# State-space x of groups 1 to 7: 32x32 blocks on VectorE and 16 transfers instead of eight TensorE transposes

## What is computed

```
xbc = silu(causal_conv(u @ w_xbc))            # x (256 channels a group), B and C (128 each)
cb   = C B^T                                  # within chunks of 64 tokens
xdt  = x * dt ;  xte = xdt * decay_to_end     # by token and head
y    = (cb * decay) @ xdt + C @ state * exp(cum) + D * x
state = exp(cum_end) * state + B^T @ xte      # from chunk to chunk
y    = rmsnorm(y * silu(z)) per group, times ssm_norm
```

## Time and profile before

| | before |
|---|---|
| device time, median of 3 runs | 1791.07 us |
| device time of the profiled execution | 1791.04 us |
| its span, first to last instruction | 1789.3 us |
| TensorE busy in the span | 99% |
| VectorE busy in the span | 54% |
| chain that ended last | 99% TensorE |
| granted TensorE clock | 1.00 over the whole span |

### The profile page before, as it was taken

The page is one execution under the profiler, slowest core; times in us unless marked ns, Lnnn a source line. Parts: engine busy times, 40 slices in busy tenths (PEclk is TensorE's granted clock), DMA queues, the critical chain, the costliest instruction groups (busy, mean ns, idle before and its releaser), DMA issues.

```text
span 1789.3 us, 26607 instructions
## 1 busy us (share of the span) xinstructions
PE 1779.4 (99%) x9956; PEld 1499.2 (84%) x9956; DVE 969.1 (54%) x1407; ACT 633.9 (35%) x1002; POOL 89.3 (5%) x92
## 2 busy tenths in 40 slices
PE   9999999999999999999999999999999999999998
PEld 7888888888888888788988888888888888888887
DVE  6444443369999989623544455565334544444333
ACT  5222322244545444422333344443222332223221
POOL 2111100000000000000000000000000011111000
PEclk9999999999999999999999999999999999999999
DMA  5323323323344443233222322322332322233332
GB/s 173 105 94 100 100 94 105 105 94 97 95 106 100 102 104 92 84 106 103 86 71 71 104 72 93 94 93 71 97 103 94 95 94 94 94 101 99 106 105 71
DMA packets 84402, 172.98 MB, mean 97 GB/s; under 512 B 36800, under 2 KB 44224, under 8 KB 84336
## 3 DMA queue, kind: packets, MB, share of 16 engines
q1 hardware_dynamic: 76288, 162.83, 29.1%
q10 hardware_dynamic: 8048, 9.24, 2.4%
HBM read 166.21 MB, written 2.16 MB: 94 GB/s over the span
## 4 chain that ended last, share of the span: by engine, by line
PE 99%; DVE 0%; DMA 0%; issue 0%; SPq 0%; ACT 0%; DVEq 0%
PE G L583 50%; PE I L583 16%; PE G L650 13%; PE G L603 8%; PE I L1085 1%; PE I L1061 1%; PE G L908 1%; PE I L1051 1%; PE I L845 1%; PE I L710 1%; PE I L854 1%; PE I L831 1%; PE I L1021 0%; PE I L1025 0%; PE I L815 0%; PE I L836 0%
## 5 line engine op out<-in xcount | busy, mean ns | idle before, releaser
L1720 DVE TENSOR_TENSOR WL<-RAW,WH 128x1024 fp32r<-128x1024 f32 x296 | 372.2, 1261 | 287.9 <-ACT WH L1182 278.5
L1182 ACT CAST WH<-RAW 128x1024 fp32r<-128x1024 f32 x295 | 306.4, 1047 | 226.1 <-PE I L583 125.8
L583 PE MATMUL G<-UH,WH 128*128 128x512 f32 x664 | 164.3, 389 | 0.0
L583 PE MATMUL G<-UL,WH 128*128 128x512 f32 x664 | 164.0, 389 | 0.0
L583 PE MATMUL G<-UH,WL 128*128 128x512 f32 x664 | 164.0, 389 | 0.0
L583 PEld LDWEIGHTS G<-UL,WH 128*128 128x128 f32 x664 | 124.6, 188 | 25.9
L583 PEld LDWEIGHTS G<-UH,WL 128*128 128x128 f32 x664 | 124.6, 188 | 25.9
L583 PEld LDWEIGHTS G<-UH,WH 128*128 128x128 f32 x664 | 124.5, 188 | 25.8
L583 PE MATMUL G<-NH,WH 128*128 128x512 f32 x448 | 113.5, 395 | 0.0
L583 PE MATMUL G<-NL,WH 128*128 128x512 f32 x448 | 110.7, 389 | 0.0
L583 PE MATMUL G<-NH,WL 128*128 128x512 f32 x448 | 110.7, 389 | 0.0
(11 more groups left out here) (355 smaller groups left out, 2618.0 us busy)
## 6 DMA issues: line engine op xcount, KB each, us to landing
RAW<-in_slabs SPq DMA_DIRECT2D x296, 512.0 KB, 3.5
cum_rows<-kept_rows ACTq DMA_DIRECT2D x16, 256.0 KB, 7.0
SU<-y_turned SPq DMA_DIRECT2D x112, 32.0 KB, 2.7
bias<-in_rel ACTq DMA_DIRECT2D x16, 128.0 KB, 3.3
bias<-in_rel ACTq DMA_DIRECT2D x16, 112.0 KB, 2.8
h<-in_x SPq DMA_DIRECT2D x6, 256.0 KB, 5.9
out_y<-h SPq DMA_DIRECT2D x4, 256.0 KB, 2.5
h<-in_x ACTq DMA_DIRECT2D x2, 256.0 KB, 3.6
```

Of the source, the lines that this page charges most:

```text
L583: ins = mm(dst, slab(W, n)[:, (k - k0) * P:(k - k0 + 1) * P], R[:, k, :], start=begin and which == 0 and k == k0, stop=end and which == 2 ...
L1182: nc.scalar.copy(slab(WH, n), RAW[:, n.slot, :]).then_inc(split_hi, 1)
L1720: V.tensor_tensor(slab(WL, n), RAW[:, n.slot, :], slab(WH, n).bitcast(F32), ALU.subtract).then_inc(split_lo, 1)
```

## The change

- `turn_x`: in rounds 1 to 7 VectorE turns the 32x32 blocks of XT right behind the silu of t = 1 (two instructions, all 256 channels) into x_turned. `move_x`: SyncE moves them with 16 transfers into x_tokens, each of 32 partitions with one piece of 1 KB. Group 0 stays with TensorE.
- TensorE has the eight transposes of x for group 0 alone. XD on ScalarE and xte, xdt on VectorE read x_tokens in SBUF instead of I01 in PSUM; xte and xdt are made by two instructions each instead of one.
- y_turned is laid out so that a transfer of `move_y` also has one piece of 1 KB. They land in y_rows; ScalarE puts them in order with the gain into SU (two instructions) and copies SU to SH (two more). `ssm_hi` moves from t = 3 to t = 2.
- `ssm_lo` of groups 0 to 6 leaves VectorE: GpSimd subtracts SH from SU in one instruction of 128x1024. The last group stays on VectorE with a semaphore of its own.
- SyncE: the 16 transfers of x stand before the loads of slabs 8 and 9 of a round, the 16 of y in one piece behind them; before, the 16 of y stood in two halves with one load between.
- TensorE waits for WH before the first third and for WL only before the last one (`need_hi`, `need_slab`).

The diff, cut to its core:

```diff
+            def move_x(g):
+                sp.wait_ge(x_blocks, g)
+                for b in range(4):
+                    for q in range(4):
+                        sp.dma_start(x_tokens[32 * q:32 * q + 32, b], x_turned[32 * b:32 * b + 32, q]).then_inc(x_moved, 16)
...
             with sp.Fori(0, NG - 2) as i:
-                for j in range(1, 6):
+                for j in range(2, 6):
                     next_load(At(ahead + j, i, 6))
-                move_y(i + 1, (0, 1))
+                move_x(i + 2)
                 next_load(At(ahead + 6, i, 6))
-                move_y(i + 1, (2, 3))
+                next_load(At(ahead + 7, i, 6))
+                move_y(i + 1, (0, 1, 2, 3))
...
             def ssm_turn(g):
...
+                if isinstance(g, int) and g == 0:
+                    for j in range(TT):
+                        for f in range(2):
+                            nc.tensor.transpose(I01[:, j * 256 + f * P:j * 256 + (f + 1) * P],
+                                                XT[:, f, j * P:(j + 1) * P], ident[:])
...
             def fm(dst, n, RH, RL):
+                need_hi(n)
+                blocks(dst, n, 0, KT, RH, RL, True, False, (0, 1))
                 need_slab(n)
-                blocks(dst, n, 0, KT, RH, RL, True, True).then_inc(slab_done, 1)
+                ins = blocks(dst, n, 0, KT, RH, RL, False, True, (2,))
+                ins.then_inc(slab_done, 1)
...
+            def turn_x(g):
+                dve.wait_ge(sems["conv_done"], after("conv_done", g, 1))
+                dve.wait_ge(x_moved, 256 * (g - 1))
+                dve.wait_ge(sems["x_copied"], after("x_copied", g - 1))
+                for f in range(2):
+                    ins = V.transpose(x_turned.rearrange("p q (j f) c -> p f j q c", f=2)[:, f],
+                                      XT[:, f, :].rearrange("p (j q c) -> p j q c", q=4, c=32))
+                ins.then_inc(x_blocks, 1)
...
+            def ssm_lo(g, at=0):
+                pool.wait_ge(sems["ssm_hi"], last("ssm_hi", g))
+                pair = bass.ds(2 * g, 2)
+                ins = nc.gpsimd.tensor_tensor(SL[:, pair, :], SU[:, bass.ds(2 * (g + at), 2), :], SH[:, pair, :].bitcast(F32), ALU.subtract)
+                ins.then_inc(sems["ssm_lo"], 2)
...
                 if not first:
-                    ssm_lo(inner - 1)
                     group_gain(inner)
```

More of the change, by code:

```diff
@@ L542, in _ @@
             norm(1)
-            with pool.Fori(0, NG - 1) as i:
+            ssm(0)
+            with pool.Fori(1, NG - 1) as i:
+                ssm_lo(i - 1)
                 ssm(i)
+            ssm_lo(NG - 2, 1)
             ssm(NG - 1)
-            pool.wait_ge(sems["ssm_lo"], last("ssm_lo", NG - 1))
+            pool.wait_ge(ssm_lo_end, 2)
             nc.gpsimd.memset(RM[:], 1.0).then_inc(gk_pool, 1)
@@ L648, in tm_tile @@
                         if j == 0 and which == 0 and k == 4:
+                            need_hi(n + 1)
+                        if j == 0 and which == 2 and k == 0:
+                            need_slab(n)
+                        if j == 0 and which == 2 and k == 4:
                             need_slab(n + 1)
@@ L1345, in ssm_copy_exp @@
             def ssm_copy_exp(g, n=None):
-                act.wait_ge(sems["xb_turned"], after("xb_turned", g))
+                initial = isinstance(g, int) and g == 0
+                if initial:
+                    act.wait_ge(sems["xb_turned"], after("xb_turned", g))
+                else:
+                    act.wait_ge(x_moved, 256 * g)
                 act.wait_ge(sems["ssm_y"], last("ssm_y", g - 1))
@@ L1478, in ssm_round @@
                         decays(0)
+                    if t == 2 and not first:
+                        ssm_hi(inner - 1)
                     if t == 3:
-                        if not first:
-                            ssm_hi(inner - 1)
                         ssm_squares(inner)
@@ L2038, in ssm_x @@
             def ssm_x(g):
[L2039 to L2044 removed]
+                initial = isinstance(g, int) and g == 0
+                if initial:
+                    dve.wait_ge(sems["x_copied"], after("x_copied", g))
+                else:
+                    dve.wait_ge(x_moved, 256 * g)
+                dve.wait_ge(sems["u_done"], last("u_done", g - 1))
+                for dst, k, name in ((XTE, 2, "xte_ready"), (XDT, 1, "xdt_ready")):
+                    if k == 1:
+                        dve.wait_ge(sems["intra_done"], last("intra_done", g - 1))
+                    if initial:
+                        ins = V.tensor_tensor(dst[:].rearrange("p j (r c) -> p (j r) c", c=CH), heads(I01[:]), rows(k),
+                                              ALU.mult)
+                    else:
+                        for s in range(2):
+                            by_tile = gsc[:, 4 * k:4 * k + 4, :].rearrange("p j (f s) -> p s (j f)", s=2)[:, s, :]
+                            ins = V.tensor_tensor(
+                                dst[:].rearrange("p j (f s b c) -> p s b (j f) c", f=2, s=2, c=32)[:, s],
+                                x_tokens[:, 2 * s:2 * s + 2],
+                                by_tile.unsqueeze(1).unsqueeze(3).to_broadcast([P, 2, 2 * TT, 32]), ALU.mult)
+                    inc(ins, name)
+            def turn_x(g):
+                dve.wait_ge(sems["conv_done"], after("conv_done", g, 1))
+                dve.wait_ge(x_moved, 256 * (g - 1))
+                dve.wait_ge(sems["x_copied"], after("x_copied", g - 1))
+                for f in range(2):
+                    ins = V.transpose(x_turned.rearrange("p q (j f) c -> p f j q c", f=2)[:, f],
+                                      XT[:, f, :].rearrange("p (j q c) -> p j q c", q=4, c=32))
+                ins.then_inc(x_blocks, 1)
             def ssm_cb(g):
```

91 lines of the change are left out of this document (51 added, 40 removed).

## The result

| | before | after |
|---|---|---|
| median of the runs, us | 1790.97 (1790.86 to 1791.34, 5 runs) | 1801.47 (1798.91 to 1803.04, 5 runs) |
| ratio to before | | 1.0057, 95% interval 1.0046 to 1.0069 |
| profiled execution, span, us | 1791.04, 1789.3 | 1801.47, 1799.7 |

The account below looks back on a forecast made before the run. VectorE's ring, 41.2 us a round, was to replace TensorE's 40.65 us as the bound. The terms +1.4 - 1.6 - 0.3 - 0.8 = -1.3 us gave 1789.7 us, with a range of 1784 to 1800 (its own 1787.5 to 1793).

Parts of the forecast that it names:

- SyncE's issue: SyncE, 32 transfers a round instead of 16: 0.42 us each and 0.05 between, 16 in 7.5 us.
- The cover for slab 10: Load behind y's transfers: lands about 0.6 us after ScalarE would take it, VectorE needs it 3.6 us after that.
- my rival for late slabs: SyncE: 0.61 us a transfer, 16 take 11.7; slab 10 lands 1.6 us late, six times: 1799 us, chance 0.06.
- The port: GpSimd's subtraction asks before VectorE's silu, which stands 2.3 us: six rounds 1803.5 us, 0.14; round 7 alone 1792, 0.04.
- VectorE's ring: VectorE's state-space round: 41.35 - 1.63 (remainder) + 1.30 (blocks of x) + 0.15 (xte, xdt) = 41.2 us, the new bound.
- TensorE's round: State product to state product: 41.52 us on average, 40.65 without the x transposes, which take 0.87 us.
- Round 1, +1.4: Round 1 gets the blocks of x and longer xte, xdt but loses no remainder: its xdt comes 1.4 us later.
- The end, -0.8: Behind the last group: TensorE's 0.79 us wait for the seventh remainder goes, 0.8 us.
- The last segment, -0.3: Before the seventh group's product: VectorE gives 1.63 - 1.30 = 0.3 us.
- ScalarE at no cost: Two more copies of 0.6 us and the move to t = 2 fit ScalarE's idle time; nothing on the path.
- Split waits at no cost: TensorE waits for no slab in this stage, so nothing to win; the added, already met waits cost nothing.
- The full gain: Rival: VectorE's ring is looser, TensorE's 0.87 us come through seven times, and the 0.79: 1784.1 us; full or most, 0.16.

Follow-up runs that it names:

- the version with both repairs: Changed kernel with y's transfers halved around slab 10's load and GpSimd's subtraction held until the silu of t = 1: 1787.94 us, ratio 0.9985.

## Why the prediction was wrong, point by point

The sum priced two things at nothing: slab 10 behind the transfers of y ("Cover: this slack"), and GpSimd's subtraction beside VectorE. Together they cost 13.5 us, from 1787.94 to 1801.47.

- **SyncE's issue, the step that failed first.** I took 0.42 us for a transfer with one piece a partition, by the slabs' 333 and the weight rows' 420 ns, and held the 608 ns of y's transfers to be the price of their eight pieces. It is 0.59 us with one piece. I had priced by the number of pieces, from rows that differed in more than that: the cheap ones come from DRAM and go to 128 or 16 partitions, those of y go from SBUF to SBUF in 32. What sets the price stays open. In the trace before, transfers from SBUF to DRAM take 0.34 to 0.44 us (medians), and one from DRAM to SBUF, issued by ScalarE, takes 0.62:

```profile
L1281 ACTq DMA_DIRECT2D cum_rows<-kept_rows x16: 602/622/728, 414.5 to 660.8; - x16
```

- **The cover for slab 10.** Its load is issued 10.65 us after the first transfer of y where I had 7.5, and VectorE stands 0.87 to 1.1 us for it. So the cover was some 2.1 us; my rival for late slabs, where 4.2 us more left 1.6, had counted with 2.6. That rival also had 11.7 us for sixteen transfers, though its own 0.61 and 0.05 make 10.6, close to what was measured. Its 1799 stood for 1.6 us a round and no collision; its cost alone was 5.2 us.
- **The port: mechanism right, place not to be had.** That the silu would stand if GpSimd asked first, and by about 2.3 us (2.2 measured), was right. No run shows the 2.3 us of its sum as such: the silu stood 2.16 us (2.85 against 0.69), and the subtraction takes 2.36 to 2.42 us unblocked, against 1.30 for half of it. That block transposes and taps leave GpSimd alone holds: in the version with both repairs the subtraction takes 2.36 to 2.38 us beside them, and they take 1.30 to 1.31 and 2.27 to 2.28 us, as without it (1.30 and 2.27 with the remainder back on VectorE). The small terms hold too: from ScalarE's end to GpSimd's start it is 0.08 us at 103.57 and 0.24 at 451.11 in the kernel before, and with register instructions between them ScalarE's first copy in the changed kernel starts 1.45 us after the start of the pair with the gain in the loop (563.17 to 564.62), without them 1.35 (735.54 to 736.89). Without the late slab GpSimd does ask within 0.03 us of the silu's start in five rounds of six (as at 562.21 and 602.84), so my 520.7 to 521.0 against 520.80 was a coin's toss, and 0.18 was too small a chance for it. Wrong was "the distance stays in every round". It does not quite, and 1.13 us after the product's start in one round and 1.10 in another are on either side of the edge. I also had only the silu in view; when the slab holds VectorE up, the product ahead of it is hit as well (565.98). The rival had all six rounds, or round 7 alone; by its own uncertainty of 0.3 us each round could fall either way, and some of them did.
- **The two rivals were treated as apart.** Each had its chance and its time. But a late slab moves VectorE against ScalarE and GpSimd, and in the profiled executions four rounds collided with the late slab and two without it.
- **VectorE's ring: 41.2 in the sum, 40.66 measured.** The listed terms were right: the remainder 1.63 (1.51 in its plain form), the blocks 1.23 to 1.30, xte and xdt +0.15 (588.61, 589.82 and 591.02 are their starts and the next one's, 2.41 us against 2.26). The term that was missing is the 0.58 us of "issue" at the loop's end, which I kept as fixed; it goes with the remainder.
- **TensorE's round: 41.52 and 40.65 in the sum, 41.31 and 40.44 measured.** 0.87 us for the transposes is exact. The average had 0.2 us a round of waiting in it, which I had read as balance. For rounds 2 to 6 the sum had -1.6 us; in the version with both repairs it is -3.5 (204.10 against 207.61 us).
- **Round 1, +1.4:** 1.40 us on VectorE's constants in the version with both repairs (462.42 against 461.02), 1.55 at the product. Right.
- **The end, -0.8:** TensorE no longer waits behind the last group. Right. The last segment, -0.3: -0.16 between the sixth and seventh product in that version, about half.
- **ScalarE at no cost:** nearly. VectorE's wait for the tanh of z is 0.38 us in the version with both repairs against 0.21, and the one in front of the turned y 0.24 (its own scaling) against 0.34. **Split waits at no cost:** right.
- **The full gain** gave 1784.1. With the two repairs it is 1787.9, 3.8 us more. In the profiled execution the first product comes 2.4 us later than that sum has it (468.36 against 466.81 - 0.87), the five rounds to the sixth take 0.8 us more (204.10 against 207.61 - 5 x 0.87), and the last segment 0.7 us. With x of group 1 left on TensorE it is 1785.6.
- **The clock** had no place in the prediction: a wait of 2 us was priced at 2 us. A fall behind it cost 1.7 us at the next product and, by the estimate above, 0.4 at the seventh.

## What to carry over

Before GpSimd gets work that reads SBUF, list what VectorE does beside it and where its inputs lie (3.31 us with both in SBUF, 1.22 with one in PSUM), then pin the place with a wait: here 8 of the 13 us lost hung on which of two engines asked first, and one wait took them back. Do not add up two mishaps that can shift each other: the late slab made two of the four collisions. Price a DMA issue by a row that is like it in source, destination, partitions and pieces (0.59 us came where rows of 0.33 and 0.42 had set the price), and put no load with a deadline behind a long series. An idle time called "issue" at a loop's end can belong to the wait in front of it (0.65 us behind one, 0.07 without): put an instruction that nobody waits for last.

## What the runs showed of the hardware

- Which of the two goes first is decided shortly before the running instruction of VectorE ends: a GpSimd instruction that asked 1.13 us into one of 1.22 us had to let VectorE's next one pass, at 1.10 us it went first. All twelve looped rounds of the two kernels whose subtraction isn't held back agree with an edge between 1.10 and 1.12 us. So VectorE's next instruction counts as having asked some 0.1 us before the end of the one that runs, an estimate from the edge and the 1.22 us.
- After a wait of 2.04 us TensorE's granted clock was 0.59 and 0.55 in the next two stretches of 2 us in the version with both repairs, and 1.00 after 2.05 us in the one with halved transfers alone; after 0.97 us, with x of group 1 on TensorE, it stayed at 1.00. In the changed kernel it falls too, behind the wait of 1.80 us at 597.79 (0.51 and 0.63). With the remainder back on VectorE one execution has four waits of 2.05 or 2.06 us, and the clock falls behind two of them (0.50 from 512 to 514 us and from 642 to 644). One fall put the next product off by 1.66 us; where VectorE's ring is the bound most of that comes back.
- VectorE's blocked instruction stands for nearly the whole of GpSimd's: 2.85 against 0.69, 3.43 against 1.22, 3.31 against 1.23 us, so 2.1 to 2.2 us longer. GpSimd's subtraction of 128x1024, where nothing blocks it, takes 2.36 to 2.42 us.
- To issue a transfer of 32 partitions from SBUF to SBUF takes 0.59 us with one piece of 1 KB a partition and 0.61 with eight pieces; the pieces hardly matter there. From issue to landing the transfers of y take a median of 2.7 us with eight pieces and a slab's load between the halves, 3.0 to 3.2 with one piece and the same load between, and 2.4 with one piece in one series; those of x take 1.8. So these runs show no gain from larger pieces there; the landing differs more with what is issued in between.
- A loop's jump on VectorE costs 0.07 us between its neighbours behind a running instruction of 1.2 us, and 0.65 us when the last instruction had to wait for VectorE's own result; the branch starts ahead of the copy in the first case (630.5 and 631.22 us) and behind it in the second (591.2 and 591.09).
